# First projection slots on unnormalised x with the root of each row applied at evacuation, and earlier banks for the output slots, in a three-layer recurrent/attention model

## What is computed

```python
def first_block(x, ...):
    xn = rms_norm(x, norm_pre_w)
    z = xn @ w_in
    ...                      # LRU over 16 blocks, windowed attention, merge
    return x + rms_norm(merged @ w_out, norm_post_w)

def second_block(x, ...):
    for l in range(2):
        h = rms_norm_2(x, norm_w[l])
        p = h @ w_in[l]
        ...                  # a: attention, b: convolution, c: gated delta rule
        y = jnp.concatenate([oa, ob, oc], axis=-1)
        x = x + y @ w_out[l]
    return x
```

## Time and profile before

| | us |
|---|---|
| median of 3 runs | 2059.43 |
| runs | 2056.8 to 2059.75 |
| the profiled execution's own time | 2059.35 |
| its span in the trace | 2057.5 |
| PE busy | 1943.2 (94%) |
| DVE busy | 1251.6 (61%) |
| ACT busy | 1094.9 (53%) |
| POOL busy | 37.2 (2%) |

### The profile page before, as it was taken

One profiled execution on the slowest core, in us unless ns is written; L12 is line 12 of the kernel. 1 busy time (PEld: TensorE's weight loads), 2 busy tenths in 40 slices (PEclk: granted clock), 3 DMA queues, 4 the chain that ended last, 5 costly groups with the idle time before them and its releaser, 6 DMA issues. The chain is left out here.

```text
span 2057.5 us, 32654 instructions
## 1 busy us (share of the span) xinstructions
PE 1943.2 (94%) x13832; PEld 1733.8 (84%) x13832; DVE 1251.6 (61%) x1726; ACT 1094.9 (53%) x1473; POOL 37.2 (2%) x42
## 2 busy tenths in 40 slices
PE   4999999999999999997899999898979999989988
PEld 4999989999888888885898998887869998988876
DVE  4887755555444445644587888545457789755442
ACT  5777755554433333344445688435444557872541
POOL 0011000000000000000000000000000000000000
PEclk9999999999999999999899999999989999999999
DMA  5454454444455555564444334213645444331153
GB/s 190 170 192 176 160 209 164 163 144 151 166 194 186 191 198 184 174 237 181 173 174 164 123 136 152 103 64 123 225 148 214 149 144 144 124 144 63 63 215 112
DMA packets 51840, 328.61 MB, mean 160 GB/s; under 512 B 7920, under 2 KB 10096, under 8 KB 13808
## 3 DMA queue, kind: packets, MB, share of 16 engines
q1 hardware_dynamic: 51696, 326.54, 43.9%
HBM read 320.23 MB, written 6.29 MB: 159 GB/s over the span
## 5 line engine op out<-in xcount | busy, mean ns | idle before, releaser
L251 DVE TENSOR_TENSOR w_lo<-w_raw,w_hi 128x2048 fp32r<-128x2048 f32 x288 | 664.2, 2307 | 457.7 <-ACT w_hi L244 457.3
L244 ACT ACTIVATE w_hi<-w_raw 128x2048 fp32r<-128x2048 f32 x288 | 551.1, 1916 | 553.4 <-PE z L278 318.4
L266 PE MATMUL z<-xn_hi,w_hi 128*128 128x256 f32 x2368 | 696.8, 294 | 6.7 <-ACT zb L1692 6.3
L266 PE MATMUL z<-xn_hi,w_lo 128*128 128x256 f32 x2368 | 671.2, 283 | 0.0
L266 PE MATMUL z<-xn_lo,w_hi 128*128 128x256 f32 x2368 | 671.2, 283 | 0.0
L266 PEld LDWEIGHTS z<-xn_hi,w_hi 128*128 128x128 f32 x2368 | 451.0, 190 | 23.0 <-issue 8.9
L266 PEld LDWEIGHTS z<-xn_lo,w_hi 128*128 128x128 f32 x2368 | 449.7, 190 | 5.2 <-issue 4.6
L266 PEld LDWEIGHTS z<-xn_hi,w_lo 128*128 128x128 f32 x2368 | 449.0, 190 | 0.0
L278 PE MATMUL z<-w_hi,xn_hi 128*128 128x512 f32 x576 | 230.1, 399 | 0.0
L278 PE MATMUL z<-w_lo,xn_hi 128*128 128x512 f32 x576 | 228.3, 396 | 0.0
L278 PE MATMUL z<-w_hi,xn_lo 128*128 128x512 f32 x576 | 228.3, 396 | 0.0
(11 more groups left out here) (389 smaller groups left out, 2016.6 us busy)
## 6 DMA issues: line engine op xcount, KB each, us to landing
w_raw<-in_w_dram SPq DMA_DIRECT2D x288, 1024.0 KB, 4.8
gate_w<-in_lru_w_dram SPq DMA_DIRECT2D x8, 512.0 KB, 5.2
x_t<-state_dram SPq DMA_DIRECT2D x2, 2048.0 KB, 7.9
x_first<-in_x_dram SPq DMA_DIRECT2D x4, 512.0 KB, 7.7
x_t<-in_x_dram SPq DMA_DIRECT2D x1, 2048.0 KB, 11.9
state_dram<-x_t SPq DMA_DIRECT2D x2, 1024.0 KB, 4.0
pw<-in_pw_dram SPq DMA_DIRECT2D x2, 1024.0 KB, 6.2
state_dram<-x_t SPq DMA_DIRECT2D x8, 256.0 KB, 2.1
```

What stands on the lines that cost most here:

```text
L244: act.activation(self.k.w_hi[:, n % SLOTS], self.k.w_raw[:, m % RAW], ACT.Copy).then_inc(self.s.rounded, 1)
L251: dve.tensor_tensor(self.k.w_lo[:, n % SLOTS], self.k.w_raw[:, m % RAW], self.k.w_hi[:, n % SLOTS].bitcast(F32), ALU.subtract).then_inc(se ...
L266: ins = pe.matmul(out, w[:, kk], x[:, kk], start=kk == 0 and j == 0, stop=kk == KT - 1 and j == 2)
```

## The change

**Unnormalised first slots.** In all three blocks the transposes read x itself and give `raw_hi` and `raw_lo`. The first four slots use these. Their results are multiplied by `root_row`, the root of each token laid along the free axis of all partitions: `spread_root` makes it by two small matmuls after slot 1, and DVE copies it to SBUF. The root itself is one ACT square root and one DVE reciprocal. GpSimd adds `raw_hi` and `raw_lo` in four chunks of 128x1024, multiplies each by `root_row`, ACT rounds the chunk to `xn_hi` and DVE makes `xn_lo`; slots from the fifth on use those, and the fifth waits for them chunk by chunk.

```diff
+def scale_chunks(pool, k, s, raw_hi, raw_lo, split):
+    for c in range(4):
+        after(pool, s.xsplit, split[c])
+        pool.tensor_tensor(k.x_whole[:, chunk(c)], raw_hi[:, chunk(c)].bitcast(F32), raw_lo[:, chunk(c)].bitcast(F32), ALU.add)\
+            .then_inc(s.whole, 1)
+    pool.wait_ge(s.rowed, 1)
+    row = k.root_row[:, None, :].to_broadcast([P, 4, T])
+    for c in range(4):
+        pool.wait_ge(s.whole, c + 1)
+        pool.tensor_tensor(k.x_whole[:, chunk(c)], k.x_whole[:, chunk(c)], row, ALU.mult).then_inc(s.xscaled, 1)
+def round_chunk(act, k, s, c):
+    act.wait_ge(s.xscaled, c + 1)
+    act.activation(k.xn_hi[:, chunk(c)], k.x_whole[:, chunk(c)], ACT.Copy).then_inc(s.chunked, 1)
+def split_chunk(dve, k, s, c):
+    dve.wait_ge(s.chunked, c + 1)
+    dve.tensor_tensor(k.xn_lo[:, chunk(c)], k.x_whole[:, chunk(c)], k.xn_hi[:, chunk(c)].bitcast(F32), ALU.subtract).then_inc(s.normed, 1)
+def spread_root(pe, k, s, split):
+    pe.wait_ge(s.rooted, 2)
+    pe.wait_ge(s.xsplit, split)
+    for m in range(2):
+        ins = pe.matmul(k.aux[0][:, P * m:P * m + P], k.root[:, m:m + 1].to_broadcast([P, P]), k.ident[:], start=True, stop=True)
+    ins.then_inc(s.spread, 1)
```

```diff
-                pe.wait_ge(s.scaled, 4)
...
+                def scale_gates():
+                    dve.wait_ge(s.used, 4)
+                    for b in range(2):
+                        dve.tensor_tensor(g_all[:, b], tile(2 + b), k.root_row[:], ALU.mult).then_inc(s.gscaled, 1)
...
                 for i in range(LRU_PASSES + 1):
                     n = 4 * i
+                    if i == 1:
+                        scale_gates()
                     if i:
                         open_gates(i - 1)
```

```diff
+                def join(c):
+                    for m in range(2):
+                        there = x_in[:, m, cols(c)]
+                        dve.scalar_tensor_tensor(out=there, in0=k.weighed[:, c, m], scalar=k.post_root[:, m:m + 1], in1=there,
+                                                 op0=ALU.mult, op1=ALU.add).then_inc(s.joined, 1)
+                if layer:
+                    split_x(3)
+                else:
+                    join(0)
+                    for c in range(4):
+                        if c < 3:
+                            join(c + 1)
+                        split_x(c)
```

```diff
         def bank_of(n):
-            return n % 3 if n < SLOT_ZB else n % 2
+            return n % 3 if n < SLOT_ZC else (n + 1) % 2
 
         def pair(c):
-            return (z[2 * (c % 2)][:, 0:Q], z[2 * (c % 2) + 1][:, 0:Q])
+            return (z[2 - 2 * (c % 2)][:, 0:Q], z[3 - 2 * (c % 2)][:, 0:Q])
...
                         if c == 0:
+                            pe.wait_ge(s.sstate, states(2))
+                        elif c == 1:
                             pe.wait_ge(s.emptied, 44)
-                        elif c == 1:
-                            pe.wait_ge(s.sstate, states(2))
```

More of the change, by code:

```diff
@@ L279, in tokens, with last_tokens @@
         ins.then_inc(self.s.used, 1)
+    def last_tokens(self, pe, n, outs, x_hi, x_lo, first_half):
+        w_hi, w_lo = (w[:, n % SLOTS].rearrange("p (k f) -> p k f", k=4) for w in (self.k.w_hi, self.k.w_lo))
+        self.await_slot(pe, n)
+        for m in range(2):
+            t = slice(P * m, P * m + P)
+            for kk in range(4):
+                row = KT - 4 + kk
+                for j, (x, w) in enumerate(((x_hi, w_hi), (x_hi, w_lo), (x_lo, w_hi))):
+                    ins = pe.matmul(outs[m], x[:, row, t], w[:, kk], start=False, stop=row == KT - 1 and j == 2)
+            ins.then_inc(self.s.used if m else first_half, 1)
     def halves(self, pe, n, half, outs, x_hi, x_lo):
@@ L468, in _, with first_squares @@
             def _(act):
[L469 to L481, removed]
+                def first_squares(h):
+                    for m in range(2):
+                        act.activation(k.junk[:, half(m, m)], x_first[:, m, half(m, h)], ACT.Square, scale=D ** -0.5,
+                                       accum_out=k.squares[:, m, h:h + 1]).then_inc(s.squared, 1)
                 act.wait_ge(s.p1_in, 16)
@@ L1237 @@
 OUT_LAST = (5, 7, 11, 15)
+OUT_TURNS = tuple(SLOT_OUT2 + i for i in (8, 10, 14))
 def layer_block(k, t, layer):
@@ new lines, in _ @@
+                for m in range(2):
+                    if layer:
+                        x, total = x_in[:, m, cols(3)], k.squares[:, m, 3:4]
+                    else:
+                        act.wait_ge(s.joined, 8)
+                        x, total = x_in[:, m], k.squares[:, m, 0:1]
+                    after(act, s.squared_x, m)
+                    act.activation(k.junk[:, 0:Q if layer else D], x, ACT.Square, scale=D ** -0.5, accum_out=total).then_inc(s.squared_x, 1)
+                act.wait_ge(s.averaged, 1)
@@ L1791, in _, with round_next @@
+                def round_next(c):
+                    if c == 0:
+                        act.wait_ge(s.weight_in, 16)
+                    for j in range(4 * c, 4 * c + 4):
+                        act.wait_ge(s.turned, KT + j + 1)
+                        act.activation(k.raw_hi[:, j], aux[j % 4][:, 0:T], ACT.Copy, scale=k.norm_w[:, j:j + 1]).then_inc(s.xrounded, 1)
                 for n in range(SLOT_OUT2 + 3, SLOTS_2):
                     ring.round(act, n + 3)
-                    if more and n in (SLOT_OUT2 + 7, SLOT_OUT2 + 9, SLOT_OUT2 + 13):
-                        square((SLOT_OUT2 + 7, SLOT_OUT2 + 9, SLOT_OUT2 + 13).index(n))
@@ L2674, in build @@
         k.eps = put("eps", [P, 1])
+        k.squares, k.mean, k.root = put("squares", [P, 2, 4]), put("mean", [P, 2]), put("root", [P, 2])
+        k.post_root, k.warm = put("post_root", [P, 2]), put("warm", [P, 1])
+        k.root_row = put("root_row", [P, T])
         k.norm_w = put("norm_w", [P, KT])
```

439 lines of the change are left out of this document (272 added, 167 removed).

## The result

The changed kernel took 2039.84 us (median of 4 runs, 2037.56 to 2039.88) against 2058.86 before, a ratio of 0.9906 (95% interval 0.9895 to 0.9918): 19.0 us faster. Forecast were 2044.7 and a range of 2018 to 2058. The profiled execution's span is 2037.9, 19.6 under that of before.

The account below looks back on a forecast made before the run. PE, busy 94% of the span, was taken as the bound, with 80.8 us of waits bearing on the change. Terms -10.4 + 3.3 + 3.9 + 16.7 + 0.6 + 0.6 won 14.7: 2059.35 to 2044.7 us, range 2018 to 2058.

Parts of the forecast that it names:

- A: Start of the first block: GpSimd's passes hold DVE up, slot 12 starts at 124.4, against 114.0; 10.4 us lost.
- B: First block to layer 0: the norm leaves the path, slot 4 ends at 1018.1 for 1021.4; 3.3 us won.
- E: The `zb` wait, 2 x 3.1 us, goes, but the k chain gives most back; 0.6 us won, bounds 0 and 6.3.
- the tail: Very end of the kernel: one half of the last addition is done under the last matmuls; 0.6 us won.
- the work between the output slots: Three turns, ACT roundings and DVE splits between output slots: costed at nothing; three splits would cost 3.6 us without cover.
- The price of a pass: One GpSimd pass over a 1024-element chunk, alternating with DVE instructions: 2.6 us; bounds no hold-up and 4.9.
- Rival 1: GpSimd's passes don't hold DVE up: 38.9 us won, 2020.5 us; chance 0.22.
- Rival 2: Each GpSimd pass waits for a whole `w_lo` and takes 4.9 us: 27.6 us more, 2072.3; chance 0.10.
- D: Opening of the output slots in two layers: banks freed earlier remove PE's 6.4 us stops and slow clock; 16.7 us won.
- Rival 3: PE still stops before the output slots, as another input is late: 2061.4 us, no measurable change; chance 0.08.
- C: Layer 0 to layer 1: 12 of 16 rows already turned, slot 4 ends 44.1 us after, now 48.0; 3.9 us won.
- the softplus chain: Start of the first block, queued on the way to slot 6: taken as 7.6 us, running from 66.8 to 74.6.

Follow-up runs that it names:

- the banks alone: The kernel before, with only the change of banks (and the wait counts and evacuation place that go with it): 2043.81 us, ratio 0.9927.

## Why the prediction was right

The direction, the mechanism and most of the terms held. The total came out 4.9 us better on the trace: A 4.7, the addresses 2.5, B 1.9, E and the tail 0.2 better, the work between the output slots 4.4 worse. That it came out so near is partly luck, since errors of both signs met.

- **The price of a pass** was taken as 2.6 us with alternation, between 0 and 4.9. Measured were 2.45 at the start and 2.94 in the layers (11.74 for four). Rival 1 (no hold-up) falls with the taps at 7.48 against 1.52 us. Rival 2 (each pass waits for a whole `w_lo`) falls too: no pass came near 4.9. The Trainium skill, in "SBUF — State Buffer", section "SBUF: two separate sides", says that the port pair of DVE and GpSimd is locked for a whole instruction and the loser fully blocks. The taps agree, 2.49 us each for 0.51, and so do the 10.9 us from moving work onto DVE. The Trainium skill's "GPSIMD Engine Reference", section 3.1, keeps elementwise work on DVE, and gives 4497 ns for 2048 elements, by which a pass would be 2.25 us, as an estimate. An addition here took 2.35 to 2.41 us at the start.
- **D**, 16.7, measured 16.7, and 16.9 for the banks alone. Rival 3 (another input is what is late) falls. Of the 3.9 that it counts for the slow clock, its rows give 1.5 for layer 1, not 1.6, and none for layer 0.
- **C**, 3.9, came out exactly by two misses of 1.0 that cancel: the row's copy was expected 22.1 us after the last matmul and stands at 21.1, and the rest took 23.0 where 22.0 was counted. Slot 4, which ends it, ran at a clock of 0.64 that no term holds. **B** was 1.9 too low: PE turns 6.4 us after the last matmul and not 4.9, behind `join`, yet the copy of the row stands 31.3 after it where 32.5 was counted, and the rest took 21.3 for 22.0.
- **A** is the term that was mis-sized: -5.7 for -10.4. Up to the taps all is within 2 us (first projection matmul 16.4 for 16.3, slots 0 to 3 end 48.0 for 49.4, taps 55.7 for 57.5, slot 4 67.8 for 68.6). The step that failed is "the softplus chain, 7.6 us", forecast from 66.8 to 74.6: it ran 64.6 to 70.0, 5.4, begun 2.2 earlier. The 7.6 were read from a chain in which two instructions stood under GpSimd's product, one in the earlier trace rows and this one behind it:

```profile
68.78 1.20 DVE L178 TENSOR_SCALAR tmp<-tmp 128x32 f32<-128x32 f32 x1
```

Without the two the chain before is 5.4 as well, and in the changed order that product comes later. The hold-up was counted in its new place and left standing in its old one. Slot 6 then follows the chain's end by 3.4 us, not 1.8, and starts at 73.4, not 76.4. Pass 1 loses 4.9, not the 6.6 counted; which part of it was over-counted is open.

- **The work between the output slots** was costed at nothing, with DVE's and ACT's spare time named. They hid theirs but for one split. The transposes are PE's own: three times 0.9 us, and for DVE's split of the group before PE stopped 1.6. That makes 4.4 us, more than the whole of C, which they were moved for. This was the prediction's plain error: cover was named for two engines, and none for the third.
- **E** was right in its sum (+0.7 for +0.6) by luck: two large numbers cancel, -3.8 and +4.5. Each holds a stop at `sq` of 3.0 us instead of 1.7; before it was in layer 1, now it is in layer 0. The slot with it took 2.9 and 4.1 us longer than in the other kernel, more than the 1.3, since it ran at a clock of 0.86 and 0.74 and not at 1.00. In both cases ACT stood 1.3 us for a weight load that landed 6.2 us after its issue where most take 4.8. In both runs of the changed kernel and all its seven variants here it is the same load in layer 0, number 195, at 6.0 to 6.3 us, so it isn't mere chance. What delays it was not tried and stays open.
- **Addresses** were not in the prediction at all: 2.5 us. Nothing in the diff's text names them.

## What to carry to other kernels

A duration read from a trace contains that trace's collisions; before it is used for a changed order, ask what stood beside it and whether that still does. Cover must be named per engine, PE's own instructions included: work moved out of a gap into a full engine costs its whole length. GpSimd isn't a free engine beside a busy DVE: four products that DVE does in 4.6 us cost it 9.8 to 11.7 when GpSimd did them.

## What was not expected of the hardware

- The step of a matmul from SBUF depends on the byte offsets of its two operands to one another: 226.7 to 234.3 ns with 512 columns, 118.4 to 120.7 with 256. Placing tensors differently, with no instruction changed, won 13.6 us of 2059 in one run. Any comparison of two kernels whose small tensors differ carries such a difference.
- At the same place of the same order the clock was not the same from run to run. Slot 4 of layer 0 ran at 1.00 after a stop of 3.21 us and again after 2.99, at 0.65 after 3.60, but at 0.67 after 2.87 and at 0.83 with a stop of 2.37 within it. It took 7.8 us at 1.00 and 9.0 to 10.0 us otherwise. After PE's stop of 7.81 us at the start the gates ran at 0.57.
